# First decays beside the projection, diagonal products between softmax pairs, values projected with their ones

## What is computed

```python
(cq, k_att, v_att, k_idx, w_idx, q_m, k_m, v_m, o_m, i_m, f_m) = split(h @ w_in)
cq = rms_norm(cq); q = rope(cq @ w_q_up); q_idx = rope(cq @ w_qidx_up); k = rope(k_att)
# 8 attention heads of 64: for each query the keys with the best index scores
idx_score[t, s] = sum_h relu(q_idx[t, h] . k_idx[s]) * w_idx[t, h]     # causal
att = softmax over the 128 chosen keys of q . k / 8, times v_att;  rms_norm per head
# 4 memory heads of 128
qk = silu(causal_dwconv(concat(q_m, k_m), conv_w (4 taps), conv_b))
b = cumsum(log_sigmoid(f_m)); key = i_m - b; top[t] = max(0, max over s <= t of key[s])
w[t, s] = exp(key[s] - top[t]) for s <= t, else 0
s_mat = (q . k / sqrt(128)) * w
h = (s_mat @ v_m) / max(|sum_s s_mat|, exp(-(top + b)));  rms_norm per head;  * sigmoid(o_m)
y = concat(att, h) @ w_out
```

## Time and profile before

| what | value |
|---|---|
| median of three runs | 3264.14 us (3261.37 to 3266.01) |
| the profiled execution | 3256.55 us, its span 3254.5 us |
| mean granted TensorE clock | 0.993 |
| TensorE matmul busy | 3130.2 us, 96% of the span, 17716 instructions |
| VectorE | 1935.6 us, 59% |
| ScalarE | 1129.7 us, 35% |
| GpSimd | 267.8 us, 8% |
| third layer: last projection product to first product of the output projection | 2031.71 to 2108.44 us |
| fourth layer: the same | 2741.51 to 2818.23 us |

### The profile page before, as it was taken

The page is one execution under the profiler, slowest core; times in us unless marked ns, Lnnn a source line. Parts: engine busy times, 40 slices in busy tenths (PEclk is TensorE's granted clock), DMA queues, the critical chain, the costliest instruction groups (busy, mean ns, idle before and its releaser), DMA issues. The chain is left out here.

```text
span 3254.5 us, 44394 instructions
## 1 busy us (share of the span) xinstructions
PE 3130.2 (96%) x17716; PEld 2580.6 (79%) x17716; DVE 1935.6 (59%) x3391; ACT 1129.7 (35%) x2021; POOL 267.8 (8%) x235
## 2 busy tenths in 40 slices
PE   6999999999999999999999899999999999999998
PEld 5998777888888798777878777777877777778886
DVE  6676657646464435667556668766555667753434
ACT  3134644111112424552222443742222534642222
POOL 0000000000000000000000028500000047400000
PEclk9999999999999999999999999999999999999999
DMA  7441114423331221127445222046544231123232
GB/s 248 132 138 64 40 53 127 136 91 100 102 117 53 69 67 56 57 85 227 149 138 161 76 86 80 24 130 194 164 135 141 65 95 56 45 79 100 87 102 78
DMA packets 317341, 337.30 MB, mean 104 GB/s; under 512 B 12048, under 2 KB 219592, under 8 KB 317136
## 3 DMA queue, kind: packets, MB, share of 16 engines
q1 hardware_dynamic: 315440, 333.65, 32.2%
q10 hardware_dynamic: 1696, 0.81, 0.1%
HBM read 330.73 MB, written 3.69 MB: 103 GB/s over the span
## 5 line engine op out<-in xcount | busy, mean ns | idle before, releaser
L2322 DVE TENSOR_TENSOR weights_low<-weights,weights_high 128x1024 fp32r<-128x1024 f32 (+5 forms) x416 | 489.6, 1178 | 737.7 <-ACT weights_high L1632 735.3
L1632 ACT ACTIVATE weights_high<-weights 128x1024 fp32r<-128x1024 f32 (+5 forms) x416 | 420.0, 1011 | 1243.7 <-PE banks L709 764.6
L1363 PE MATMUL banks<-h_high,weights_high 128*128 128x512 f32 (+1 forms) x1760 | 656.6, 373 | 21.4 <-DVE h_low L2334 13.6
L1363 PE MATMUL banks<-h_low,weights_high 128*128 128x512 f32 (+1 forms) x1760 | 649.4, 369 | 0.0
L1363 PE MATMUL banks<-h_high,weights_low 128*128 128x512 f32 (+1 forms) x1760 | 649.2, 369 | 0.0
L709 PE MATMUL banks<-weights_high,h_high 128*128 128x512 f32 (+4 forms) x1288 | 484.1, 376 | 16.7 <-DVE h_low L2334 8.0
L709 PE MATMUL banks<-weights_high,h_low 128*128 128x512 f32 (+4 forms) x1288 | 472.7, 367 | 0.0
L709 PE MATMUL banks<-weights_low,h_high 128*128 128x512 f32 (+4 forms) x1288 | 471.2, 366 | 0.0
L1363 PEld LDWEIGHTS banks<-h_high,weights_high 128*128 128x128 f32 x1760 | 332.6, 189 | 88.8 <-DVE h_low L2334 15.2
L1363 PEld LDWEIGHTS banks<-h_high,weights_low 128*128 128x128 f32 x1760 | 332.5, 189 | 56.4
L1363 PEld LDWEIGHTS banks<-h_low,weights_high 128*128 128x128 f32 x1760 | 332.8, 189 | 52.6
(11 more groups left out here) (437 smaller groups left out, 4040.4 us busy)
## 6 DMA issues: line engine op xcount, KB each, us to landing
weights<-in_w_gate_up SPq DMA_DIRECT2D x88, 512.0 KB, 3.8
projected<-in_w_mod SPq DMA_DIRECT2D x40, 1024.0 KB, 6.0
weights<-in_w_down SPq DMA_DIRECT2D x80, 512.0 KB, 3.8
extra<-in_w_mod SPq DMA_DIRECT2D x37, 1024.0 KB, 6.5
weights<-in_w_in SPq DMA_DIRECT2D x48, 512.0 KB, 3.6
weights<-in_w_gate SPq DMA_DIRECT2D x44, 512.0 KB, 4.6
weights<-in_w_up SPq DMA_DIRECT2D x44, 512.0 KB, 3.8
weights<-in_w_mod SPq DMA_DIRECT2D x32, 512.0 KB, 4.0
```

The costliest lines, as they stand in the source:

```text
L1363: mm = pe.matmul(bank[:, 0:cnt], wt[:, k, :], x[:, k, a - GOFF:a - GOFF + cnt], start=(k == 0 and q == 0), stop=(k == KD - 1 and q == 2))
L1632: act.activation(WH[s_ % 2][:, 0:k * n], slots[j % LAND][:, 0:k * n], ACT.Copy).then_inc(S["w_high"], 1)
L2322: dve.tensor_tensor(WL[s_ % 2][:, 0:k * n], slots[split_of[s_] % LAND][:, 0:k * n], WH[s_ % 2][:, 0:k * n].bitcast(F32), ALU.subtract).the ...
```

## The change

1. `M_O` and `M_V` change places in `projected`, whose rows grow by four columns. The copies of the M_V group write the four heads 129 columns apart, so `VA` becomes a view of `projected`; GpSimd only sets the ones, before the softmax.
2. The rows for `TOPS[0]` are saved and read back ten weight loads earlier, without the wait for the query rotation. VectorE, no longer GpSimd, adds the mask for head 0, in slot 22, and ScalarE computes the decays of head 0 in slots 24 and 25 (`first_decays`).
3. Block 5 is transposed in slot 20 and taken by ScalarE in slot 21. GpSimd does its first tap too, and begins as soon as the first scores are out. The other blocks' order and steps change, seven in place of eight.
4. The four diagonal products go one by one into steps 12, 13, 14, 15 of the softmax; the diagonals are built in step 9.
5. The dummy products are dropped. The first scores wait for banks 0 and 2 alone, and the wait for all projection copies comes behind them.
6. ScalarE's SiLUs behind the softmax begin with blocks 0 and 4, one instruction each.

```diff
-W2 = 3408
+W2 = 3412
-A_K, A_V, M_Q, M_K, M_V, M_O = 336, 848, 1360, 1872, 2384, 2896
+A_K, A_V, M_Q, M_K, M_O, M_V = 336, 848, 1360, 1872, 2384, 2896
...
+    def projected_to(t, a, n, bank):
+        if second and a == M_V:
+            return pr(t, a, 516).rearrange("p (h e) -> p h e", e=129)[:, :, 0:128], bank[:, 0:n].rearrange("p (h e) -> p h e", e=128)
+        return pr(t, a, n), bank[:, 0:n]
...
-        CONV_TURNED = {1: 5, 4: 0, 6: 6, 7: 4, 9: 7, 10: 1, 11: 3, 12: 2}
+        CONV_TURNED = {1: 6, 3: 0, 4: 7, 6: 4, 8: 2, 9: 3, 11: 1}
+        DIAGONAL_STEPS = {12: 0, 13: 1, 14: 2, 15: 3}
...
-        TOPS = [SC[:, 13408:13920]] + ...
-        MD = [P[:, 16264:16776]] + ...
+        TOPS = [GB[:, 1280:1792]] + ...
+        MD = [X[:, 1280:1792]] + ...
-        DT_FIRST = EX[:, 0:1280]
+        DT_FIRST = [GB[:, 3072:3584], GB[:, 3584:3968], GB[:, 1792:2048], GB[:, 1024:1152]]
-        VA = SC[:, 11344:11344 + 2064].rearrange("p (t h e) -> p t h e", t=4, e=129)
+        VA = PW[:, :, M_V:M_V + 516].rearrange("p t (h e) -> p t h e", e=129)
...
 TensorE, slot 20
+                    pe.wait_ge(S["kept_act"], 5 * LAT_T)
+                    turn_aside("a", [pr(t, M_Q + 128 * BY_POOL[0], 128) for t in OUT_T])
...
 TensorE, softmax
-                    warm(2)
-                B.all_emptied(pe)
+                    for i in (0, 2):
+                        PB6.free(pe, i)
+                    CV.append(conv_banks())
...
                 scores(0)
-                if not second:
+                if second:
+                    PB6.all_emptied(pe)
+                else:
                     gates(10)
...
+                        if p in DIAGONAL_STEPS:
+                            conv_by_diagonals(DIAGONAL_STEPS[p])
...
 TensorE, memory heads
-                conv_by_diagonals()
-                for i in range(2):
+                for i in (0, 2):
                     CV[0].free(pe, i)
...
 SP
-                if second and j == first_out:
+                if second and j == first_out - 10:
                     sp.wait_ge(S["row_tops"], 1)
                     sp.dma_start(w["tops"], TOP[1][:, 256:768]).then_inc(S["tops_saved"], 16)
-                if second and j == first_out + 2:
+                if second and j == first_out - 8:
                     sp.wait_ge(S["tops_saved"], 16)
-                    sp.wait_ge(S["query_rope"], LAT_T)
...
 GpSimd
+                pool.memset(VA[:, :, :, 128:129], 1.0).then_inc(S["v_ones"], 1)
                 for f in BY_POOL:
-                    if f == BY_POOL[1]:
-                        pool.wait_ge(S["first_tops"], 16)
-                        masked(0)
-                    pool.wait_ge(S["conv_taken"], TAKEN_BY[f])
+                    if f == BY_POOL[0]:
+                        pool.memset(CP[f][:, 0:3], 0.0).then_inc(S["v_ones"], 1)
+                        pool.wait_ge(S["v_ones"], 2)
+                        pool.wait_ge(S["mix_scores"], 1)
+                        step(pool.tensor_scalar(QK[:, f, :], CP[f][:, 0:512], ..., ALU.mult, ALU.add))
+                    else:
+                        pool.wait_ge(S["conv_taken"], TAKEN_BY[f])
...
                 pool.wait_ge(S["mix_out"], group_of(units, len(units) - 1) + 1)
-                pool.memset(VA[:, :, :, 128:129], 1.0).then_inc(S["v_ones"], 1)
-                pool.tensor_copy(VA[:, :, :, 0:128], PW[:, :, M_V:M_V + 512]...).then_inc(S["v_ones"], 1)
...
 ScalarE
+            def first_decays(rows):
+                act.wait_ge(S["ml_masked"], 1)
+                for s_ in rows:
+                    key, to = T16[:, s_, 0:1], DT_FIRST[s_]
+                    ins = act.activation(to[:, 0:128], MD[0][:, 128 * s_:128 * (s_ + 1)], ACT.Exp, scale=-1.0, bias=key)
+                    if s_ < LAT_T - 1:
+                        ins = act.activation(to[:, 128:512 - 128 * s_], TOPS[0][:, 128 * (s_ + 1):512], ACT.Exp, scale=-1.0, bias=key)
+                    ins.then_inc(S["ml_exp"], 1)
...
                 elif slot == 21:
                     side.empty(act, "d", "a")
+                    kept(CP[BY_POOL[0]][:, 3:515], side.empty(act, "a", "a"))
...
                 elif slot in (24, 25):
                     for f in (2 * (slot - 24), 2 * (slot - 24) + 1):
                         kept(KTT[:, f, :], side.empty(act, "a", "a"))
+                    first_decays((2 * (slot - 24), 2 * (slot - 24) + 1))
...
-                act.wait_ge(S["mix_scores"], len(units) // 2)
-                memory_decays(0)
-                conv_silu(4, 8, 2, 3)
-                conv_silu(0, 1, 2, 3)
+                conv_silu(0, 1, 2, 0)
+                conv_silu(4, 5, 2, 0)
+                conv_silu(5, 8, 2, 3)
                 conv_silu(1, 2, 3, 3)
                 conv_silu(3, 4, 3, 4)
...
 VectorE, beside the projection
+                    elif slot == 22:
+                        dve.wait_ge(S["first_tops"], 16)
+                        dve.tensor_tensor(MD[0]..., TOPS[0]..., CN[:, C_LATE:C_LATE + 128]..., ALU.add).then_inc(S["ml_masked"], 1)
```

More of the change, by code:

```diff
@@ L423, in conv_banks @@
     def conv_banks():
[L424 removed]
+        return Banks([PS[3], PS[6], PS[1]], "conv_filled", S, {"a": "conv_taken"})
     def conv_turned_beside(p):
@@ L433, in decayed @@
         n = 512 - 128 * s_
-        return DT[g % 2][:, 0:n] if h else DT_FIRST[:, ml_at[s_]:ml_at[s_] + n]
+        return DT[g % 2][:, 0:n] if h else DT_FIRST[s_]
     def norm_turned_banks():
@@ L542, in layer @@
         SQUARES = [P[:, 15240:15752], EX[:, 1536:2048]]
-        TOPS = [SC[:, 13408:13920]] + [EX[:, 2048 + 512 * h:2560 + 512 * h] for h in range(1, ML_H)]
-        MD = [P[:, 16264:16776]] + [SC[:, 6736 + 512 * i:7248 + 512 * i] for i in (1, 0)]
+        TOPS = [GB[:, 1280:1792]] + [EX[:, 2048 + 512 * h:2560 + 512 * h] for h in range(1, ML_H)]
+        MD = [X[:, 1280:1792]] + [SC[:, 6736 + 512 * i:7248 + 512 * i] for i in (1, 0)]
         MD.append(MD[1])
         DT = [SC[:, 7760 + 512 * i:8272 + 512 * i] for i in range(2)]
-        DT_FIRST = EX[:, 0:1280]
+        DT_FIRST = [GB[:, 3072:3584], GB[:, 3584:3968], GB[:, 1792:2048], GB[:, 1024:1152]]
         PTT = [SC[:, 8784 + 1280 * i:10064 + 1280 * i] for i in range(2)]
-        VA = SC[:, 11344:11344 + 2064].rearrange("p (t h e) -> p t h e", t=4, e=129)
+        VA = PW[:, :, M_V:M_V + 516].rearrange("p t (h e) -> p t h e", e=129)
         OUT = [PSA[:, 2048 + 1024 * i:3072 + 1024 * i].rearrange("p (n e) -> p n e", e=256) for i in range(2)]
@@ L1011, in conv_turned, with conv_by_diagonals @@
                 mm.then_inc(CV[0].filled, 1)
[L1013 to L1019, removed]
+            by_diagonals = []
+            def conv_by_diagonals(j):
+                if j == 0:
+                    pe.wait_ge(S["diagonals"], 1)
+                    by_diagonals.append(CV[0].fill(pe, "a"))
+                mm = pe.matmul(by_diagonals[0][:, :], DIAG[:, j, :], CP[BY_PE][:, j:j + 512], start=(j == 0), stop=(j == 3))
+                if j == 3:
+                    mm.then_inc(CV[0].filled, 1)
             def softmax_attention():
@@ L1096, in softmax_attention @@
                 if second:
-                    warm(2)
-                B.all_emptied(pe)
+                    for i in (0, 2):
+                        PB6.free(pe, i)
+                    CV.append(conv_banks())
+                else:
+                    B.all_emptied(pe)
+                scores(0)
                 if second:
-                    CV.append(conv_banks())
-                scores(0)
-                if not second:
+                    PB6.all_emptied(pe)
+                else:
                     gates(10)
@@ L1156, in mlstm_attention @@
                     if g == 0:
-                        pe.wait_ge(S["v_ones"], 2)
+                        pe.wait_ge(S["v_ones"], 1)
                     elif (h, s_) == (1, 0):
@@ L1570, in _ @@
                 side.skip("d")
+                side.skip("a")
                 for n in range(LAT_T):
@@ L1583, in _ @@
                 for f in BY_POOL:
-                    if f == BY_POOL[1]:
-                        pool.wait_ge(S["first_tops"], 16)
-                        masked(0)
-                    pool.wait_ge(S["conv_taken"], TAKEN_BY[f])
+                    if f == BY_POOL[0]:
+                        pool.memset(CP[f][:, 0:3], 0.0).then_inc(S["v_ones"], 1)
+                        pool.wait_ge(S["v_ones"], 2)
+                        pool.wait_ge(S["mix_scores"], 1)
+                        step(pool.tensor_scalar(QK[:, f, :], CP[f][:, 0:512], VT[:, V_CWT + f:V_CWT + f + 1], VT[:, V_CB + f:V_CB + f + 1], ALU.mult, ALU.add))
+                    else:
+                        pool.wait_ge(S["conv_taken"], TAKEN_BY[f])
                     for j in (1, 2, 3):
@@ L1854, in taken @@
             def taken(f):
-                bank, i = conv_bank(), (BY_DVE + (BY_PE,)).index(f) if f in BY_DVE + (BY_PE,) else 0
+                bank, i = conv_bank(), BY_DVE.index(f) if f in BY_DVE else 0
                 if i >= 2:
```

(12 more changed lines are left out.)

15 lines of the change are left out of this document (8 added, 7 removed).

## The result

The changed kernel takes 3265.69 us (median of 12 runs, 3259.84 to 3272.28), the kernel before, beside it, 3258.36 (12 runs): a ratio of 1.0019 over all runs, 95% interval 1.0011 to 1.0027, or 6 us slower, where I had forecast 1.9 us faster. The twelve times of the kernel before lie in two groups, six at 3255.3 to 3256.6 us and six at 3260.1 to 3266.0, so a median of three, like the 3264.14 that the forecast starts from, can be 6 us off. The profiled execution took 3263.1 us (span 3261.2), against 3256.55.

What follows compares the result with a forecast made beforehand. TensorE, with 96% of the span, was taken to bound the kernel. Terms of -2.16 - 0.54 + 1.13 + 0.4 + 0.2 = -0.97 us a layer, -1.9 for two, took 3264.14 to 3262.2 us; range 3254 to 3269.

Steps and rivals of the forecast that it cites:

- head: Softmax start, last projection product to first maximum: without dummies and with fewer waits, the maximum starts 2.16 us earlier a layer.
- transposes: One convolution block's transposes leave the softmax loop for slot 20, where a later stop hides them: -0.54 us a layer.
- diagonals in the loop: Four diagonal products moved into softmax steps 12 to 15, a full loop: 3.52 less 0.27 idle, +3.25 us a layer.
- behind the loop, with GpSimd's masks: After T, the issue's end of the last softmax values: 3.52 saved less a 1.40 us VectorE wait; GpSimd's mask sums +0.2.
- slot 22: Projection slot where VectorE's mask sum meets GpSimd's rotation, which TensorE waits for: +0.4 us a layer, bounds 0 and 0.7.
- early decays, memory heads: Decays moved to slots 24 and 25, hidden in ScalarE's 3.88 us wait; memory heads' later stops stay: 0 each.
- clock: TensorE's granted clock at the new stops of 1.3 and 1.4 us: no loss in the sum, 0.
- third rival: Clock falls at the new stops without dummies: four falls of 1.7 us, 6.8 in all, 3269.0 us; chance 0.09.
- the rope stop: TensorE's 1.39 us projection wait for GpSimd's last query rotation; followed by full-speed products, cited against a clock fall.
- a granted clock under 1 in the softmax: Sign listed as showing the forecast wrong: TensorE's granted clock below 1 in the softmax; no size given.

Runs made afterwards that it cites:

- e1: Changed kernel with one 512-column dummy product put back in the stop between first and second scores; timed 3.3 us under the kernel before.
- e4: Changed kernel with one dummy product in that stop and all four diagonal products behind the softmax loop; timed 3.6 us under the kernel before.
- after: The changed kernel itself, no dummy products and four diagonal steps in the loop; 3265.69 us, timed 6.2 us over the kernel before.
- e2: Kernel before with only its two dummy products at the softmax's head left out; timed 3.6 us over the kernel before (-0.3 to 7.5).
- e6: Changed kernel with one dummy product of 128 columns in the first stop; timed 3.3 us over the kernel before (-0.3 to 6.8).
- e9: Changed kernel with one dummy product in the stop, two diagonal steps in the loop and two behind; timed 8.5 us under the kernel before.
- e7: Kernel before with one dummy product at the head in place of two; timed 1.6 us under the kernel before (-5.9 to 2.6).
- e10: Changed kernel with one 512-column dummy product ahead of the first scores, none in the stop; timed 0.3 us under the kernel before (-3.3 to 2.9).
- e5: Changed kernel with one dummy in the stop and VectorE's squares moved behind the first memory head; timed 1.3 us under the kernel before (-4.6 to 2.0).
- e8: The changed kernel run again, unedited; timed 5.5 us over the kernel before (1.6 to 9.1).
- e3: Changed kernel with the diagonal products behind the softmax loop and no dummy products; timed 1.6 us over the kernel before (-1.3 to 4.9).

## Why the prediction was wrong

By its own steps, a layer, with e1 as the change at full clock:

| step | forecast | measured | from |
|---|---|---|---|
| head | -2.16 | -2.25 | 3.75 to 1.50 |
| transposes | -0.54 | -0.89 | loop of e4 against before |
| diagonals in the loop | +3.25 | +2.64 | e1 against e4 |
| behind the loop, with GpSimd's masks | -2.12 + 0.2 | -2.09 | 26.72 to 24.63; chain's end at T + 2.86 as before |
| slot 22 | +0.4 | +0.25, fourth layer +0.40 | GpSimd's lag |
| early decays, memory heads | 0 | 0 | split's idle 0.97; same stops 0.46, 1.02 |
| clock | 0 | +4.77 | after against e1 |

Without the last line the sum is -2.3 (fourth layer -2.2), better than the forecast's -0.97. The time of e1, -3.3 us (-5.9 to -0.3), fits two such layers, though it does not rule out the forecast's -1.9. (The -0.89 holds some 0.4 us of a shorter second stop, 0.29 for 0.72 at the head, besides the transposes.) The diagonals were overpriced twice: the loop of e1 has 3.19 us more of busy TensorE than e4's, not 3.52, and it swallows 0.55 us of idle (1.41 to 0.86), not the 0.27 of the last 16 us.

The step that failed is the clock, which the sum puts at nothing and the third rival turns down. I saw the stops and that no dummies cover them, and gave the fall a chance of 0.09, setting against it that "the 1.39 us stop of the earlier trace rows is followed by full-speed products". That compared the length of two stops and not what surrounds them: the rope stop lies among dense products of 512 columns, this one among products of 64 by 128 and transposes. That the surroundings are why the clock holds at the one and falls at the other fits e1, e2 and e6; no run changed the rope stop to show it. The price was wrong too. I took 0.28 x 6 = 1.7 us from the earlier trace rows; a fall here is 5.1 us of lost clock, and 4.8 of it is paid, since TensorE is busy for 98% of e1's loop (47.15 of 48.01). Two falls of 4.8 are 9.5 us; the prediction had four of 1.7, 6.8 in all. The sign "a granted clock under 1 in the softmax" was listed under what would show it wrong, and it did. The Trainium skill's rule that I cited (TensorE: Matmul & The Clock Gate, "What's actually happening": activity releases the throttle) agrees with e1, e2 and e6 in that a full product in the stop held the clock, and with none or a short one it fell. The prediction spoke of an idle TensorE; here it had been busy for 1.07 of the 2 us before the fall and for 0.98 of the microsecond in which it fell.

That 3265.69 lies inside the forecast's range, 3254 to 3269, is luck: the range stood on the 3264.14 of three runs. From the 3258.36 measured beside the change the same forecast would be 3256.5, 9.2 us too low.

Both stretches and slot 22 give +5.0 us (2.18 + 2.21 + 0.25 + 0.40); the two profiled executions differ by 6.55. Of the remaining 1.5 us, 0.6 was there by 1959 us, ahead of slot 22. The clock lost outside the stretches, 0.8 us more in the profile after by the estimate above, would be half of it; the rest is not settled.

## What to carry to other kernels

A dummy product that lies ahead of a stop has two prices: its own time and the clock that it holds; before it is dropped, look at what TensorE does in the microseconds around it, not at the longest idle time. Where an engine stands anyway, a dummy there can cost nothing (e1: it filled a 1.35 us stop up to 0.30, and the second scores were no later). And of work that could sit in a full loop, as much belongs behind it as fills the stop there (e9: two of four steps). Compare the same stretch in both traces: falls of the clock elsewhere can move a whole execution by more than the change does.

## What was unexpected of the hardware

The clock falls while TensorE is busy, not in the stop: at 2036 to 2037 it is 0.98 busy and granted 0.70. And heads with the same instructions differ: with one dummy ahead of the scores the clock held in one layer and fell in the other (e7, e10), and the falls of e2 lasted 13 and 7 us. Falls come and go as well in the first block, which is the same in all versions (0.90 and 1.00 at 500 to 550). With e1's dummy in the stop it held in all eight layers profiled (e1, e4, e5, e9); with no dummy at all it fell in all eight (after, e8, e2, e3). Why one layer falls and its like does not, no run here shows.
